# Gathering expert rows six experts ahead, and moving the wait for the adds into the overflow loop

## The reference

```
(silu(x @ w_gate[e]) * (x @ w_up[e])) @ w_down[e]
```

## Time and profile before

| | us |
|---|---|
| median of 3 runs | 1740.0 |
| lowest and highest | 1735.1, 1740.9 |
| the profiled execution | 1737.9 |
| its span, first to last instruction | 1736.0 |
| TensorE busy in the span | 1534.2 (88%) |
| VectorE busy | 871.1 (50%) |
| ScalarE busy | 444.2 (26%) |
| GpSimd busy | 109.5 (6%) |

### The profile page before, as it was taken

One profiled execution on the slowest core, in us unless ns is written; L12 is line 12 of the kernel. 1 busy time (PEld: TensorE's weight loads), 2 busy tenths in 40 slices (PEclk: granted clock), 3 DMA queues, 4 the chain that ended last, 5 costly groups with the idle time before them and its releaser, 6 DMA issues. The chain is left out here.

```text
span 1736.0 us, 38991 instructions
## 1 busy us (share of the span) xinstructions
PE 1534.2 (88%) x16348; PEld 1081.1 (62%) x16348; DVE 871.1 (50%) x1878; ACT 444.2 (26%) x873; POOL 109.5 (6%) x134
## 2 busy tenths in 40 slices
PE   4999999958999999999949999979993988988893
PEld 3888888834676666666745555545552766666661
DVE  2445545454767777787654555527773122111110
ACT  2222222221323323233103333324442111111110
POOL 0000000000000000000000000000000122333320
PEclk9999999978999999999868999989996999999997
DMA  9422222553213112121115352439531999999961
GB/s 325 150 85 90 85 85 91 195 182 107 77 48 118 47 65 72 44 65 44 52 44 131 101 132 67 127 115 364 197 146 44 360 321 330 321 321 319 320 190 18
DMA packets 101278, 260.27 MB, mean 150 GB/s; under 512 B 34192, under 2 KB 53280, under 8 KB 91648
## 3 DMA queue, kind: packets, MB, share of 16 engines
q1 hardware_dynamic: 93376, 240.64, 40.4%
q0 software_dynamic: 7744, 17.33, 4.4%
HBM read 206.04 MB, written 60.56 MB: 154 GB/s over the span
## 5 line engine op out<-in xcount | busy, mean ns | idle before, releaser
L526 PEld LDWEIGHTS a_ps<-a_hT,a_wz 128*128 128x128 f32 x1792 | 202.6, 192 | 3.8 <-issue 3.8
L526 PE MATMUL a_ps<-a_hT,a_wz 128*128 128x128 f32 x1792 | 204.0, 275 | 0.0
L1885 PE MATMUL d_ps<-wo,d_oT 128*128 128x512 f32 x288 | 131.1, 605 | 0.8 <-DVE d_oT L1705 0.8
L2053 DVE COPY f_xT<-f_turned 128x384 f32<-128x384 f32 x32 | 17.8, 558 | 185.5 <-PE f_turned L2020 185.5
L1885 PEld LDWEIGHTS d_ps<-wo,d_oT 128*128 128x128 f32 x288 | 53.5, 193 | 59.7 <-issue 58.2
L1464 ACT ACTIVATE c_probs<-c_score,c_top 128x1024 f32<-128x1024 f32 (+8 forms) x72 | 50.5, 702 | 124.9 <-DVEq L1442 119.0
L2046 PE MATMUL f_down<-wd,f_midT 128*96 128x512 f32 x160 | 79.7, 645 | 1.8 <-DVE f_midT L2065 1.8
L2251 DVE TENSOR_SCALAR f_y<-f_down,table 96x512 f32<-96x512 f32 x32 | 23.9, 747 | 107.6 <-PE f_down L2046 107.6
L2258 ACT ACTIVATE f_xT<-f_turned 128x384 f32<-128x384 f32 x32 | 15.7, 490 | 223.7 <-PE f_turned L2020 223.7
L822 DVE TENSOR_TENSOR b_M<-b_ps,r_causal 128x512 f32<-128x512 f32 x72 | 46.4, 686 | 51.7 <-PE b_ps L1163 51.2
L1102 PE MATMUL b_ps<-b_wg,r_hT 128*128 128x512 f32 x128 | 67.4, 640 | 0.0
(11 more groups left out here) (362 smaller groups left out, 2900.3 us busy)
## 6 DMA issues: line engine op xcount, KB each, us to landing
wgu<-w_gate_up SPq DMA_DIRECT2D x20, 2048.0 KB, 18.3
f_wgu<-w_gate_up SPq DMA_DIRECT2D x12, 2048.0 KB, 19.1
wd<-w_down SPq DMA_DIRECT2D x20, 1024.0 KB, 12.6
f_wd<-w_down SPq DMA_DIRECT2D x12, 1024.0 KB, 14.0
zm_d<-a_zm SPq DMA_DIRECT2D x9, 896.0 KB, 4.5
r_zm<-zm_d SPq DMA_DIRECT2D x9, 896.0 KB, 6.8
r_hT<-hT_d SPq DMA_DIRECT2D x14, 512.0 KB, 4.2
b_hT<-hT_d SPq DMA_DIRECT2D x13, 512.0 KB, 4.0
```

The lines of the kernel that those rows point to most:

```text
L526: mm = pe.matmul(banks[Z_BANKS[n % 2]][:, j * P:(j + 1) * P], wz[:, i, (g + j) * P:(g + j + 1) * P], hT[t % 2][:, i, :], start=(i == 0), s ...
L1885: mm = pe.matmul(banks[2 + u][:], oT[t % 2][:, HB * branch(u) + k, :], wo[:, HB * branch(u) + k, half(u)], start=(k == 0), stop=(k == HB - 1))
```

## The change

The loop of POOL now calls gather(e+6) at the top of turn e, before it waits for y, instead of gather(e+4) behind the add. Gathers 4 and 5 are issued ahead of the loop. The number of row buffers stays four. The index tile of gather e was last used by add e-8, so a wait for that add is put into gather. In overflow the wait for all adds moves from ahead of the loop into its body, and POOL gets the same wait behind the loop.

```diff
     AHEAD = 4
+    LEAD = AHEAD + 2
...
         def overflow(eng, work):
 
-            for j in range(2):
-                eng.wait_ge(added[j], 16 * (NE // 2))
             eng.wait_ge(plan_ready, 1 + START)
             eng.wait_ge(slot_in, 16 + START)
             used = eng.value_load(plan[0:1, OVERFLOW:OVERFLOW + 1], min_val=0, max_val=OVERFLOW)
             with eng.Fori(0, OVERFLOW) as n:
                 with eng.If(n < used):
+                    for j in range(2):
+                        eng.wait_ge(added[j], 16 * (NE // 2))
                     work(n)
...
                 if e >= AHEAD:
                     pool.wait_ge(s["turn_done"], e - AHEAD + 1 + START)
+                if e >= LEAD + 2:
+                    pool.wait_ge(added[e % 2], 16 * ((e - LEAD) // 2))
...
             pool.memset(one[:], 1.0).then_inc(one_set, 1)
+            for e in range(AHEAD, LEAD):
+                gather(e)
             for e in range(NE):
+                if e + LEAD < NE:
+                    gather(e + LEAD)
                 pool.wait_ge(s["y_dve"], e + 1 + START)
...
-                if e + AHEAD < NE:
-                    gather(e + AHEAD)
                 if 0 <= e - 10 < 2 * NT:
                     scatter(e - 10)
             overflow(pool, work)
+            for j in range(2):
+                pool.wait_ge(added[j], 16 * (NE // 2))
```

## The result

| | before | after |
|---|---|---|
| median of the runs, us | 1739.2 (4 runs) | 1717.8 (4 runs) |
| lowest and highest | 1735.1, 1740.9 | 1712.8, 1721.4 |
| the profiled execution | 1737.9 | 1714.4 |
| its span | 1736.0 | 1712.5 |

The ratio is 0.988, with a 95% interval from 0.9861 to 0.9899: about 21 us faster. I take the 23.5 us between the two spans apart. The first rows are the waits of TensorE in the changed kernel between 1355 and 1680 us (total, times, longest).

A forecast was written before the change was run, and what follows sets the result against it. Late gathers held up TensorE, with nearly full DMA engines and the weights' landings next in line. 1737.9 - 19.9 (gathers further ahead) - 4.0 (tail) = 1714.0 us, range 1700 to 1731.

The forecast's parts named there:

- The bound behind the gathers: Expert stretch: once the 33.6 us of gather waits go, TensorE follows the weights' landings from some expert past the middle.
- the chain: Rival in the expert stretch: add landings of 19.7 to 21 us set the pace, up to 1733.9 us; chance 0.20.
- part 1: Gathers further ahead in the expert stretch: gain 19.9 us, with ends of 13.2 and 31.2.
- landing at 1674.0: Expert 31's gate-up weights land at 1674.0 instead of 1676.2, from -6.7 + 4.5 = -2.2 us.
- expert 31 starts right behind it: Expert 31's first gate product follows its weights' landing at 1674.0 at once, instead of coming at 1693.93.
- half of the idle time filled: DMA engines up to expert 31's landing: deeper queues fill half of 13.5 us idle, moving the landing by -6.7 us.
- part 2: Tail: with the wait for adds inside the loop body, engines enter the empty overflow loop earlier; taken as 4 us.
- it starts 3.7 us earlier, or 5.1: POOL's overflow loop starts 3.7 us earlier, or 5.1 if its sequencer goes on while descriptors are written.
- Near 17: Sign in the tail: the span ends near 17 us after the last add has landed, under 21.
- The slower case: Rival: add landings beyond 21.0 us; with two more waits 25.3 us, 13.4 per expert, 1795 us in all; chance 0.06.
- a longer wait for adds: Rule against the change: gathers issued apart may need their own wait behind weights, 6.7 us, so adds land later.
- 46.6 us: Time lost from expert 2 to 31 against 9.68 us per expert: 33.6 in gather waits, 13.0 in what follows them.

The follow-up runs named there:

- lighter loads: Changed kernel with down weights of experts 5 to 31 loaded only in their first half: 1688.2 us; the kernel before with the same loads left out: 1699.3 us.
- the shorter queue: Changed kernel with the weight loads of expert e+5 issued one expert later, four experts' weights in flight at most: 1719.1 us, ratio 0.9891 to the kernel before.

## Why the prediction was right, and where it was not

**The bound behind the gathers: right.** The waits for gathers went, the adds did not become the chain (12.7 us to land; 19.7 would have bound), and TensorE ran into the weights. The lighter loads show it, since 26 us went from the stretch with half a MB less per expert. The second half was foreseen as the place of the waits; they begin earlier, at expert 12. Loads were to take 30 to 40 us and took 42 to 44.

**The size of part 1: too large, 19.9 for 13.1 us.** The step that failed is "landing at 1674.0", and with it "expert 31 starts right behind it". The landing came at 1675.0, but on a clock that started 2.0 us earlier, so at 1677.0 on that of the kernel before: 2.9 to 3.0 us later than my estimate. The term that was mis-sized is "half of the idle time filled", -6.7 us. Up to 30 us ahead of the landing the share did rise from 0.96 to 0.99, which is worth some 8 us; but then it fell to 0.65 where it had been 0.84, and 5.7 us of it were lost again. The prediction took the mean share of all engines for the time of a landing, and a landing waits for the last of its 16 steps. The other 3.8 us were put at nothing, in "right behind it": 0.9 at expert 28, and 2.9 in the last three experts, whose loads came faster than TensorE's 9.68 us, so that it could no longer stay right behind them. 19.9 - 3.0 - 3.8 = 13.1.

**The size of part 2: too small, 4.0 for 8.4 us.** The failed step is "it starts 3.7 us earlier, or 5.1": POOL's sequencer didn't wait for the descriptors of the last add, it even loaded the number of blocks 0.15 us before that add's work began, so 5.4 us were won there, more than the 4 that was taken. The views of the loop's line do show the turns, against what I wrote; they would have shown that POOL's loop and its drain are the end. The 3.0 us of the faster loop could not have been read from them. "Near 17" from the last landing to the end was 12.2.

**The sum.** The profiled executions differ by 23.5 us, and I had 23.9; but the near hit is in part luck. Part 1 was 6.8 us too large and part 2 was 4.4 too small, 3.0 of that by the accident of the loop's code, and 2.0 us are no gain: 23.9 - 6.8 + 4.4 + 2.0 = 23.5. By medians the gain is 21.3 us, close to the 13.1 + 8.4 of the two parts, and 1717.8 lies inside the range. The slower case, more than one extra wait of the adds, did not show at all. The Trainium skill (DMA: Bandwidth & Descriptors, Queues, rings and completion order) has an engine alternate between its queues a whole packet at a time, and the prediction took from it a longer wait for adds. They took 0.8 us more and gathers about 2 less, so one more wait did not come; whether the 0.8 is that rule at work no run here tells apart.

## What to carry to other kernels

When waits for one transfer are taken away, look at the next landing in line and compute the end from it; most of 46.6 us went to a bound that nothing had waited for before. Estimate that landing from the slowest part of a load and not from the mean share of the DMA engines. A small prefetch can be late while big ones are far too early, and then an issue one turn earlier, at the top instead of the bottom of the loop, can get all that more depth would, as it did here. At the end of a kernel, let the engine that finishes last wait for as little as possible, and put a branch around a loop that is mostly empty.

## What the runs showed of the hardware

- A 2 MB load lands in 16 steps that can lie far apart: of expert 31's in the changed kernel half had come after 16.5 us and the last after 38.8, while the DMA engines were 0.65 busy in the last 30 us.
- Empty turns of a loop cost 0.75 us each on TensorE (17.6 us from the load of the number of blocks to the end of 22 turns) and 0.44 or 0.6 us on POOL, with the same instructions, depending on the code ahead of them.
- POOL's last DRAIN took 6.6 us in ten of twelve experiments' kernels and both others, whether it started 0.25 us behind the last landing or 13.9 us, and 7.6 to 7.7 us when it started ahead of it.
- In the changed kernel TensorE stood still inside the up products in three places (1.9 to 2.8 us each), waiting for nothing that the profile names; in each, a 16 KB packet of code loading overlaps the gap, though such packets come every 10 us or so anyway. One of them:

```profile
1560.15 2.67 PE L2036 MATMUL f_upped<-f_xT,wgu 128*64 128x96 f32 x60
1565.58 0.59 PE L2036 MATMUL f_upped<-f_xT,wgu 128*64 128x96 f32 x4 [2.76 <-issue]
```

The kernel before had 0.9 us of this, the changed one 7.4 (with a fourth pause of 0.5), the one with lighter loads 1.3, and the one with the shorter queue still 6.7. Over all profiles with full loads it was 4.1 to 8.8 us with the early gathers and at most 1.2 with the old ones. That code arrives late behind the weights would fit, but it wasn't tried by itself and stays open.
